# Routed stages with 112 slots per unit in place of 128

## The reference

```python
# first block, twice: 16 experts in 4 groups, 256 hidden columns each; a token goes to ONE group
g_p, g_sel = lax.top_k(g_prob, 1)                       # group
top_p, top_i = lax.top_k(e_prob, MOE_TOP_K)             # two of its four experts
for e in range(MOE_EXPERTS):
    hid = jax.nn.silu(t @ w_gate[e]) * (t @ w_up[e])
    y = y + gate[:, e:e + 1] * (hid @ w_down[e])
# second block, once: 8 experts, 3584 hidden columns each; a token goes to TWO experts
for e in range(N_EXPERTS):
    y = _swiglu(h, w_gate[e], w_up[e], w_down[e])
    out = out + gates[..., e:e + 1].astype(h.dtype) * y
```

## Time and profile before

| | |
|---|---|
| median of 3 runs | 2142.24 us (2141.05 to 2142.54) |
| span of the profiled execution | 2140.5 us |
| PE matmuls, busy | 2077.1 us, 97% |
| PE weight loads, busy | 1700.6 us, 79% |
| DVE, busy | 1700.4 us, 79% |
| ACT, busy | 1418.6 us, 66% |
| DMA over the span | 281 GB/s |
| m0 / m1 / ff / m2 run from about | 212 to 360 / 514 to 661 / 823 to 1010 / 1178 to 2135 us |

### The profile page before, as it was taken

One profiled execution on the slowest core, in us unless ns is written; L12 is line 12 of the kernel. 1 busy time (PEld: TensorE's weight loads), 2 busy tenths in 40 slices (PEclk: granted clock), 3 DMA queues, 4 the chain that ended last, 5 costly groups with the idle time before them and its releaser, 6 DMA issues.

```text
span 2140.5 us, 30902 instructions
## 1 busy us (share of the span) xinstructions
PE 2077.1 (97%) x10092; PEld 1700.6 (79%) x10092; DVE 1700.4 (79%) x2276; ACT 1418.6 (66%) x1889; POOL 130.8 (6%) x122
## 2 busy tenths in 40 slices
PE   8999999999998999999899999999999999999998
PEld 7876787867887887887776888888888888888887
DVE  4755998747997657445776999999999999999996
ACT  5662885444884634444442888888888888888885
POOL 1000100001000001111110100000000000000000
PEclk9999999999999999999999999999999999999999
DMA  7317895426993455551342899999999999999995
GB/s 275 136 74 288 345 411 197 170 91 236 412 393 107 184 219 212 200 199 74 136 177 99 319 380 384 374 381 386 368 390 378 381 377 389 370 385 380 365 404 198
DMA packets 88343, 601.60 MB, mean 281 GB/s; under 512 B 10336, under 2 KB 10400, under 8 KB 19776
## 3 DMA queue, kind: packets, MB, share of 16 engines
q1 hardware_dynamic: 79744, 570.40, 67.4%
q0 software_dynamic: 8512, 30.05, 4.6%
HBM read 585.11 MB, written 15.30 MB: 281 GB/s over the span
## 4 chain that ended last, share of the span: by engine, by line
PE 84%; DVE 9%; ACT 3%; DMA 2%; issue 2%; POOL 0%; DVEq 0%; SPq 0%; ACTq 0%; POOLq 0%
PE bank L512 24%; PE bank L514 24%; PE bank L513 24%; PE bank L1055 2%; PE bank L1515 2%; PE bank L639 1%; DVE gu_lo L1877 1%; DMA ffw_gu<-in_gate_up_m 1%; PE bank L2995 1%; DVE pj_lo L549 1%; PE bank L453 1%; DVE small L393 1%; DVE dn_lo L1877 1%; PE bank L1557 1%; DMA pieces<-in_pieces 1%
## 5 line engine op out<-in xcount | busy, mean ns | idle before, releaser
L1877 DVE TENSOR_TENSOR gu_lo<-ffw_gu,gu_hi 128x1024 fp32r<-128x1024 f32 x620 | 754.4, 1235 | 93.1 <-ACT gu_hi L1692 79.0
L1692 ACT CAST gu_hi<-ffw_gu 128x1024 fp32r<-128x1024 f32 x620 | 649.2, 1052 | 84.8 <-PE bank L514 45.3
L512 PE MATMUL bank<-gu_hi,xg_lo 128*128 128x512 f32 x1152 | 461.3, 400 | 0.0
L514 PE MATMUL bank<-gu_hi,xg_hi 128*128 128x512 f32 x1152 | 450.5, 391 | 0.0
L513 PE MATMUL bank<-gu_lo,xg_hi 128*128 128x512 f32 x1152 | 449.6, 390 | 0.0
L1877 DVE TENSOR_TENSOR dn_lo<-ffw_d,dn_hi 128x1024 fp32r<-128x1024 f32 x299 | 365.2, 1229 | 26.5 <-ACT dn_hi L1700 17.1
L1700 ACT CAST dn_hi<-ffw_d 128x1024 fp32r<-128x1024 f32 x310 | 326.5, 1056 | 63.1 <-PE bank L514 56.0
L512 PE MATMUL bank<-dn_hi,hidt_lo 128*128 128x512 f32 x664 | 260.1, 392 | 6.3 <-DVE hidt_lo L1877 6.1
L514 PE MATMUL bank<-dn_hi,hidt_hi 128*128 128x512 f32 x664 | 258.5, 389 | 0.0
L513 PE MATMUL bank<-dn_lo,hidt_hi 128*128 128x512 f32 x664 | 258.4, 389 | 0.0
L514 PEld LDWEIGHTS bank<-gu_hi,xg_hi 128*128 128x128 f32 x1152 | 216.2, 188 | 45.8
(11 more groups left out here) (444 smaller groups left out, 2692.2 us busy)
## 6 DMA issues: line engine op xcount, KB each, us to landing
ffw_gu<-in_gate_up_m SPq DMA_DIRECT2D x288, 1024.0 KB, 7.1
ffw_d<-in_down_m SPq DMA_DIRECT2D x144, 1024.0 KB, 9.0
pieces<-in_pieces SPq DMA_DIRECT2D x70, 1024.0 KB, 6.9
ffw_gu<-in_gate_up_ff SPq DMA_DIRECT2D x22, 1024.0 KB, 6.8
ffw_d<-in_down_ff SPq DMA_DIRECT2D x11, 1024.0 KB, 8.7
h<-token_sums POOLq DMA_DIRECT2D x3, 1024.0 KB, 7.4
pieces<-in_pieces SPq DMA_DIRECT2D x4, 512.0 KB, 8.0
norm_vec<-in_ln_g POOLq DMA_DIRECT2D x4, 512.0 KB, 4.5
```

Of the source, the lines that this page charges most:

```text
L512: nc.tensor.matmul(bank, a_lo, b_hi, start=start, stop=False)
L514: return nc.tensor.matmul(bank, a_hi, b_hi, start=False, stop=stop)
L1692: nc.scalar.copy(gu_hi[:, 2 * k:2 * k + 2, :], ffw_gu[:, blk["slot"], 2 * k:2 * k + 2, :])\
L1877: return V.tensor_tensor(out, x, hi.bitcast(F32), ALU.subtract)
```

## The change

`SLOTS` becomes 112. All stationary operands of the routed products, PSUM areas, copies and both indirect DMAs use 112 rows or columns; the tiles keep their places and strides. The flag compares with 112. The overflow branch, which handles 128 rows a round, gets a second round in its body (`OV_FROM`): rows 112 to 239, then 240 and above. The dense stage ff keeps 128 (`rows_of`). The diff, cut to its core:

```diff
-            g.indirect_dma_start(out=row_x, out_offset=None, in_=token_rows, in_offset=slot_rows(u))\
+            g.indirect_dma_start(out=row_x[0:SLOTS], out_offset=None, in_=token_rows, in_offset=slot_rows(u))\
...
-    SLOTS = P
+    SLOTS = 112
+    OV_FROM = (SLOTS, SLOTS + P)
...
+    def rows_of(st):
+        return P if st["col"] is None else SLOTS
...
-                last = three_products(psum[st["par"]], x(c), (gu_hi[:, c, :], gu_lo[:, c, :]), c == 0, c == DC - 1)
+                last = three_products(psum[st["par"]][0:n], x(c), (gu_hi[:, c, :], gu_lo[:, c, :]), c == 0, c == DC - 1)
...
-            last = nc.tensor.transpose(psum[2][:, at:at + P], hid[:, st["par"], f * P:(f + 1) * P], ident)
+            last = nc.tensor.transpose(psum[2][:, at:at + n], hid[0:n, st["par"], f * P:(f + 1) * P], ident[0:n, 0:n])
...
-                last = three_products(psum[3 + 2 * st["tile"] + half],
-                                      (hidT_hi[:, st["par"], f, :], hidT_lo[:, st["par"], f, :]),
+                last = three_products(psum[3 + 2 * st["tile"] + half][0:n],
+                                      (hidT_hi[:, st["par"], f, 0:n], hidT_lo[:, st["par"], f, 0:n]),
...
-            last = nc.tensor.transpose(psum[5 + c // 4][:, (c % 4) * P:(c % 4 + 1) * P],
-                                       row_x.rearrange("t (p c) -> t c p", c=DC)[:, c, :], ident)
+            last = nc.tensor.transpose(psum[5 + c // 4][:, (c % 4) * P:(c % 4) * P + SLOTS],
+                                       row_x[0:SLOTS].rearrange("t (p c) -> t c p", c=DC)[:, c, :], ident[0:SLOTS, 0:SLOTS])
...
-            return lambda c: (hi[:, c, :], lo[:, c, :])
+            return lambda c: (hi[:, c, 0:SLOTS], lo[:, c, 0:SLOTS])
...
-        nc.scalar.copy(hidT_hi[:, st["par"]].rearrange("p f t -> p (f t)"),
-                       psum[2][:, st["par"] * BLK:(st["par"] + 1) * BLK]).then_inc(sem("hidt_hi_ready"), 1)
+        nc.scalar.copy(hidT_hi[:, st["par"], :, 0:n], turned_hidden(st, n)).then_inc(sem("hidt_hi_ready"), 1)
...
-            nc.scalar.copy(xg[side][0][:, 4 * k:4 * k + 4, :].rearrange("p c t -> p (c t)"), psum[5 + k])\
+            nc.scalar.copy(xg[side][0][:, 4 * k:4 * k + 4, 0:SLOTS], turned_rows(k))\
...
-            with dve.Fori(0, n_units) as u:
+            for turn, start in enumerate(OV_FROM):
+                with dve.Fori(0, n_units) as u:
+                    v = n_units * turn + u
...
```

More of the change, by code:

```diff
@@ L809, in add_sums @@
             pool.wait_ge(sem("sums_copied"), q0 - r + u + 1)
-            g.indirect_dma_start(out=token_sums, out_offset=slot_rows(u), in_=unit_sums, in_offset=None, compute_op=ALU.add)\
+            g.indirect_dma_start(out=token_sums, out_offset=slot_rows(u), in_=unit_sums[0:SLOTS], in_offset=None, compute_op=ALU.add)\
                 .then_inc(sem("scratch_moved"), 16)
@@ L1544, in gather_tensor @@
                 for part, src in enumerate((tok_lo, tok_hi)):
-                    last = nc.tensor.matmul(psum[5 + half], pick_t[:, j, :], src[:, j, cols],
+                    last = nc.tensor.matmul(psum[5 + half][0:SLOTS], pick_t[:, j, 0:SLOTS], src[:, j, cols],
                                             start=(j == 0 and part == 0), stop=(j == T - 1 and part == 1))
@@ L1576, in scatter_tensor @@
             for part, src in enumerate((yg_lo, yg_hi)):
-                last = nc.tensor.matmul(psum[banks[half]], pick_r[:, j, :], src[:, half * 512:(half + 1) * 512],
+                last = nc.tensor.matmul(psum[banks[half]], pick_r[0:SLOTS, j, :], src[0:SLOTS, half * 512:(half + 1) * 512],
                                         start=(part == 0), stop=(part == 1))
@@ L1728, in row_x_scalar, with turned_rows @@
             act.wait_ge(sem("gathered"), 2 * ROUTER[t] + half + 1)
-            nc.scalar.copy(row_x[:, half * 512:(half + 1) * 512], psum[5 + half]).then_inc(sem("row_x_ready"), 1)
+            nc.scalar.copy(row_x[0:SLOTS, half * 512:(half + 1) * 512], psum[5 + half][0:SLOTS]).then_inc(sem("row_x_ready"), 1)
+    def turned_rows(k):
+        return psum[5 + k].rearrange("p (c t) -> p c t", c=4)[:, :, 0:SLOTS]
     def rows_hi_scalar(act, q, side):
@@ L1741, in sums_copy_scalar @@
         for half in range(2):
-            ins = nc.scalar.copy(unit_sums[:, half * 512:(half + 1) * 512], psum[3 + half])
+            ins = nc.scalar.copy(unit_sums[0:SLOTS, half * 512:(half + 1) * 512], psum[3 + half][0:SLOTS])
         ins.then_inc(sem("sums_copied"), 1)
@@ L1948, in sums_lo_vector @@
             cols = slice(half * 512, (half + 1) * 512)
[L1949 removed]
+            last = rest(yg_lo[0:SLOTS, cols], psum[3 + half][0:SLOTS], yg_hi[0:SLOTS, cols])
         last.then_inc(sem("yg_split"), 1)
@@ new lines, in overflow_tensor, with block_of @@
+            for turn in range(len(OV_FROM)):
+                with pe.Fori(0, n_units) as u:
+                    v = n_units * turn + u
+                    pe.wait_ge(dve, ov_at("dve", t, v, 0, 4))
+                    pe.wait_ge(sem(f"ov_load_{t}"), 16)
+                    for last in gather_matmuls():
+                        pass
+                    last.then_inc(done, 1)
+                    pick_turn_tensor(P)
+                    permute_tensor(pe, done, P)
+                    def block_of(b):
+                        pe.wait_ge(dve, ov_at("dve", t, v, b, 8))
+                        pe.wait_ge(sem(f"ov_load_{t}"), 16 + 48 * (nb * v + b + 1))
+                        for c in range(DC):
+                            last = nc.tensor.matmul(psum[0], ov_x[:, c, :], ov_gate_up[:, c, :], start=(c == 0), stop=(c == DC - 1))
+                        last.then_inc(done, 1)
+                        pe.wait_ge(dve, ov_at("dve", t, v, b, 9))
+                        for f in range(2):
+                            last = nc.tensor.transpose(psum[2][:, f * P:(f + 1) * P], hid[:, 0, f * P:(f + 1) * P], ident)
+                        last.then_inc(done, 1)
+                        pe.wait_ge(dve, ov_at("dve", t, v, b, 10))
+                        for half in range(2):
+                            for f in range(2):
+                                last = nc.tensor.matmul(psum[3 + half], ov_hidT[:, f, :],
+                                                        ov_down[:, f, half * 512:(half + 1) * 512], start=(f == 0), stop=(f == 1))
+                        last.then_inc(done, 1)
+                    ov_blocks(pe, t, block_of)
+                    pe.wait_ge(dve, ov_at("dve", t, v, nb, 8))
+                    for k in range(4):
+                        last = nc.tensor.matmul(psum[(3, 4, 5, 6)[k]], pick_r[:, k // 2, :].bitcast(F32),
+                                                ov_y[:, (k % 2) * 512:(k % 2 + 1) * 512], start=True, stop=True)
+                    last.then_inc(done, 1)
```

164 lines of the change are left out of this document (73 added, 91 removed).

## The result

The kernel after takes 2158.32 us (median of 4 runs, 2157.05 to 2159.04); the kernel before, on the same chip, 2142.39 (4 runs, 2141.05 to 2142.55). The ratio is 1.0081, with an interval of [1.0069, 1.0092]: 15.9 us slower. The profiled execution took 2157.05 us with a span of 2155.2, against 2140.5 before.

What follows compares the result with a forecast made beforehand. PE was taken as the bound, its 227 ns beat set by 512 moving columns. Products, turns, copies and jump at 0, first blocks 0.6 and stage ends 0.1 gave 0.7 us less than 2142.24: 2141.5, range 2137.0 to 2143.2.

Steps and rivals of the forecast that it cites:

- Products at 0: 5184 routed matmuls with 112 stationary columns: no change, since the 188 ns load lies beside the 227 ns beat; bound 4.4 us gain.
- a narrow operand that costs time: Case that narrower stationary operands make the kernel slower in a way no row shows; no size given, chance 0.03.
- The load is part of the beat: Rival: routed matmuls also pay for loaded columns, 0.86 ns less each; 4.9 us less in all, 2137.3; chance 0.11.
- Turns at 0: Block pairs and eight turns per unit: no change, because the load of 128 columns sets their pace.
- twin of -5.6: Rival: turns go by their moving columns, 13.5 ns less each, 5.6 us in all; time 2135.9, chance 0.04.
- The sign given for the turns: If turns go by moving columns, m2's pairs stand 8.39 us apart for 8.41, with a unit boundary below 9.31.
- Copies at 0: ACT and DVE copies of turned blocks get 28 and 33 ns shorter, hidden in m2 behind gate/up products: no change.
- First four blocks, -0.3 a stage: Start of m0 and m1, where DVE and a ffw_gu load carry the chain: 0.3 us less a stage, 0.6 for both.
- 64 KB less, which is 0.16 us: The 112-row gather beside the ffw_gu load in m0 and m1 saves 0.16 us if the load waits behind it.
- The longer jump at 0: End of each routed stage: engines jump over an overflow branch with a body twice as long, at no cost.
- The longer jump is paid: Rival: DVE waits for code fetches behind the overflow branch at three stage ends, 3.9 to 7.8 us; 2145.4 to 2149.3, chance 0.05.
- The change doesn't do what it says: Rival: a unit above 112 rows runs both overflow rounds, 245 us more in m0 alone, above 2380; chance 0.01.

Runs made afterwards that it cites:

- e1: Kernel before with only the routed products' stationary operands narrowed from 128 to 112 columns: 2153.88 us against 2140.88, ratio 1.0063.
- e12: Kernel before with all turns of the routed stages (block pairs and eight per unit) on 112 rows and columns: 2140.11 us against 2141.2, ratio 0.9994.
- e5: Kernel before with only the pair of turns of each routed block on 112 rows and columns: 2138.51 us against 2142.05, ratio 0.9985.
- e9: Kernel before with only the two indirect DMAs of the routed stages on 112 rows: 2147.93 us against 2141.2, ratio 1.0033.
- e2: Changed kernel with all widths back at 128, so only the overflow branch's second round (never run) differs from before: 2145.11 us, ratio 1.002.
- e4: Kernel after with both indirect DMAs and the copy into unit_sums back on 128 rows: 2155.62 us, ratio 1.0059 to the kernel before.

## Why the prediction was wrong

2141.5 us was forecast with a range up to 2143.2, and "slower" had 0.08. The measured 2158.3 lies above the range.

- **Products at 0: the step that failed.** "I cost it at 0", with a bound of 4.4 us of gain, and "in the other direction nothing shows a narrower operand to be dearer". That sentence set the bound of a loss at nought only because no row spoke. Measured alone: 13.0 us by the medians, 10.4 in m2 (e1). The failing thought was that a load with room to spare beside the stream (188 ns of 227) can change nothing when it shrinks. The only rows of a narrow operand, 114 against 120 ns, had 256 moving columns, and extending them to 512 had the sign wrong. The text did say where it would break, "if the beat of 227 ns moves at all: 1 ns of it is 5 us", and the 0.03 for a narrow operand that costs time was far too low.
- **"The load is part of the beat".** Wrong as well: the load fell by 13 ns with 112 columns and by 54 with 64, and the beat rose. *Why* it rises stays open: with the load the number of PSUM rows written changed too, and no run parts them. The Trainium skill ("TensorE: Matmul & The Clock Gate", section "Back-to-back issue gap") says that the spacing of a stream is set by both operations; the runs agree so far as a change of the stationary operand alone moved the beat. The Trainium skill ("TensorE: Matmul & The Clock Gate", section "Weight-path perf modes") names a faster weight load for exactly 128 columns of a type other than FP32; the loads show no step at 128 (184 ns at 124, 188 at 128, on the line of 0.83 ns a column), and 124, 112 and 120 columns in that order of cost are not explained by it. The rival's counter-argument took a plain fp32 matmul, 429 ns, for "two passes of 512 columns"; no row shows that it is two.
- **Turns at 0, with a twin of -5.6.** Half right. The row turns are at 0 (e12). The pairs gain 1.8 us in m2 (e5), 8 ns a turn (the 13 ns a block and 6.7 a turn in the expectation of e12 are too small), and 3.9 beside narrow products (943.5 against e1's 947.4), of which some 1.2 are nine blocks fewer in the dear pattern. The sign given for the turns, 8.39, should have been 8.38 (two turns of 13.5 ns). The reasoning held for turns in a row, and was applied to pairs that stand between products.
- **Copies at 0.** Their durations fell as forecast (hidt_lo 383 ns for 384), all covered in m2. No run measured them alone.
- **First four blocks, -0.3 a stage.** The term of hidt_lo is as told (0.33 to 0.30 on the chain). The other, "64 KB less, which is 0.16 us", has the wrong sign: bytes were priced, and the 4 KB rows of a 112-row gather each take some 30 to 60 ns longer. It costs 3.3 us over m0 and m1 in the kernel after and some 3.5 in e9. What in the 112 rows does it is open; the records don't tell which engine or partitions a packet belongs to. The Trainium skill ("DMA: Bandwidth & Descriptors", section "The descriptor swizzle") shows a transfer to 128 partitions divided so that each engine writes one port; no run here shows whether 112 rows break that division.
- **The longer jump at 0.** The rival "The longer jump is paid" was real, and its price near the lower bound: 4.2 us by the medians of e2, 3.0 at one clock, for 3.9 to 7.8. Its place was wrong. DVE waits only 0.38 us more. It is PE's branch that takes some 2.5 us longer, and the text had waved that off with "PE has filler behind it": the filler itself starts late, ends at 368.81, and only then come the turns of the next stage at 368.65, which DVE had made ready at 366.12 + 1.28 = 367.40. So the turns start 1.25 us after they could. Not all of it reaches the path: PE then waits 0.96 us for `xm_lo` where it waited 1.62, and the first product of od starts at 370.65 for 367.90, 2.75 us later, of which 2.05 were there at the last pair of turns of m0. The jump costs 0.7 us there and 1.7 at the end of the kernel; behind m1 a stretch of lower clock in the kernel before hides it. The instruction queue carried 56 packets for 53, so the earlier trace rows could not tell it either way. The other 3.0 us of od lie behind it: 1.3 arise before 411.62 us of before, where the chain waits for a load of `pieces` that takes 8.33 us for 7.10 (the delay there varies from -0.1 to 1.9 us between the kernels, with one round or two, and its cause is open), and 1.7 come with the stretch at 0.50 from 416.80 us.

```profile
367.90 0.46 PE L512 MATMUL bank<-pj_hi,xm_lo 128*128 128x424 f32 x1 [1.62 <-DVE xm_lo L494]
```

```profile
370.65 0.46 PE L512 MATMUL bank<-pj_hi,xm_lo 128*128 128x424 f32 x1 [0.96 <-DVE xm_lo L494]
```

- **"The change doesn't do what it says"** did not come in: no overflow round ran.

By the medians the parts give 13.0 (e1) + 4.2 (e2) + 6.7 (e9) - 3.5 (e5) = 20.4 us, and 15.9 were measured. Read at one mean granted clock each, they are some 11.2 (e1, at 0.995, two runs; the two others give 11.7 and 15.5) + 3.0 (e2) + 3.4 (e9) - 1.9 (e5) = 15.7, and 13.6 with the 2.1 us more that the turns gain in company. The kernel after, at 0.993 and 0.994, is 13.6 and 13.1 us above the runs of before with these clocks (one and five). So the parts add up to within a us or so, which is what a clock given to a thousandth allows (a step of it goes with some 1.9 us), and the rest of the 15.9 goes with a lower clock in the runs of the kernel after.

## What to carry to other kernels

A tuned loop of matmuls has a beat, not a sum of costs: when an operand gets narrower, measure the beat at the new width before the change is spread over the kernel, since less work in a full-size tile can run slower. Price a smaller indirect DMA by its packets and not its bytes, and look for what it runs beside. When two kernels differ by a few us, compare runs of the same granted clock before you add up parts. Code that never runs costs at the place that jumps over it: keep it short or off the path of the engine whose filler or next stage waits behind the branch.

## What the runs showed of the hardware

- fp32r products with 512 moving columns in a stream: 226.7 ns apart with 128 stationary columns, and in m2 longer by 0.9 ns a matmul with 124, 5.5 with 120, 2.6 with 112, 2.5 with 96 and 2.3 with 64. With 112 the same instructions run in one of two patterns, 226/229/232 or 231/232/237.
- The weight load takes 188, 184, 181, 174, 161 and 134 ns at these widths, and 141 for 139 and 203 for 191 where a turn's load has 112 rows in place of 128.
- An indirect gather of 112 rows of 4 KB in m0 and m1: 192 to 220 ns a row, for 159 to 162 with 128 rows, and a 1 MB half of `ffw_gu` beside it lands after 14.9 to 15.1 us for 12.9 to 13.9. The indirect add takes 327 ns a row with either.
- Compare-and-branch of PE over the body of one round: less than 0.4 us to 1.6 us, and 3.3 to 3.8 over a body of twice the length.
- After 2.18 us without a matmul the granted clock fell to 0.73 over the next 3 us in e2, and after 2.60 us to 0.67 in e4; after 2.71 us it stayed at 1.00 in the kernel after.
- Runs of one kernel spread from 2137.8 to 2145.1 us, and follow their mean granted clock, 0.997 to 0.993.
